# Windowed attention of the second layer: probabilities scaled ahead of their transposes, outputs kept turned

## The chip, the cores and the metric

One NeuronCore of a Trainium2 chip runs the whole program in one launch. The metric is the device time of one execution in microseconds (us), as the median of several timed runs; lower is better. A separate execution is profiled, and all rows shown come from it.

## What is computed

A trunk of two decoder layers over 1024 tokens of width 1024, in float32. Layer 0 mixes by retention and by dilated attention, layer 1 by sliding-window attention with grouped heads and learned sinks; each layer ends in an MLP with a squared ReLU. The change lies in the mixer of layer 1:

```
h = rmsnorm(x, norm_mix[1])
q, k, v = split(h @ w_qkv + b_qkv)          # 16 query heads, 4 key/value heads, 64 wide
q, k = rope(rmsnorm(q)), rope(rmsnorm(k))
s = q . k / 8, keys at distance 0..127 only
m = max(max over keys of s, sink)
p = exp(s - m);  den = sum(p) + exp(sink - m)
o = (p @ v) / den                           # 16 heads side by side: 1024 columns
x = x + o @ w_out1
```

## The kernel before

**Tiles.** The tokens lie on the 128 partitions in T = 8 tiles. Every projection is a float32 product made of three single-pass products of high and low parts (hi x hi, lo x hi, hi x lo), so each left operand stands turned, with the model's columns on the partitions, in `hT_hi` and `hT_lo`.

**The second attention stage** is `s_slots`, one function of that name on each engine, all written out by hand as a pipeline over slots t. There are 4 groups of heads (one key/value head with its four query heads) by 8 token tiles, 32 pairs p = (group, tile). Slot t makes the projection of pair t (24 matmuls of 128x384, `gemm_steps`), and at the same time the later steps of earlier pairs. Each engine runs its instructions in the order written, and waits on semaphores:

- TensorE: 12 of the 24 projection matmuls, then `trans(t-3)`, which turns the probabilities, `scores(t-2)`, `values(t-4)`; then the other 12 matmuls, `backs(t-4)` and `heads_T(t-1)`, which turns the queries and the key.
- ScalarE: `head_squares(t)`, in four of eight slots the high half of a weight split, `copy_O(t-4)`, `probs_T(t-3)` (turned probabilities out of PSUM), `probs` for the first half of pair t-2 (exponentials), `probs` for the second half, `heads_T_copy`.
- VectorE: `bias_G(t)` (evacuates the projection), `outputs(t-5)`, in four of eight slots `split_lo` (the low half of a weight split), `sums(t-1)` (sums of the squares), `maxima` of the first half of pair t-2 (mask, maximum, sink), `prep(t-1)` (norm and rotation), `maxima` of the second half.
- GpSimd: `gains(t)`, `keep_V(t-3)`, `head_rstd(t-1)` (a power to -1/2 of five numbers, L1949).

`values` multiplies V by the turned probabilities and so gives the output turned (head columns on the partitions, `o_ps`). Before, `copy_O` writes it to `Pm`, `backs` turns it back with two transposes, and `outputs` multiplies it by 1/den into `X`. For the output projection the finished tile of `X` is then turned again: `mixed_T` (eight transposes a tile, six tiles inside the slots from t = 30 on, and two more by `tile_T` in `out_proj`), copied and split by `copy_half` and `lo_half`.

In the first slots of a group a pair's keys are only one block wide (`width` is 128 in place of 256), so slots with t = 2, 3, 4 modulo 8 have less work on TensorE. From t = 32 on the slots carry the first column block of the output projection; `X` is loaded again from `x_spill` for the residual.

The lines that the prediction steps on: L498 to L500 projection matmuls, L567 transposes of probabilities, L615 scores, L644 values, L603 transposes back, L541 transposes of the finished tile, L651 turned heads; on ScalarE L1010 and L1013 exponentials, L1020 and L1022 copies of the turned heads, L965 squares; on VectorE L1647 evacuation, L1588 to L1592 `outputs`, L1636 `split_lo`, L1500 `sums`, L1574 to L1582 `maxima`, L1509 to L1526 `prep`; on GpSimd L1933 `gains`, L1949 the power.

Of the kernel before, what the change touches and what calls it, by code (L numbers as in the profile page):

```python
# [29 lines left out]
def hybrid_trunk(nc, x_in, positions, norm_mix, norm_mlp, w_up, w_down, w_in, w_out0, gn_gain, dq_gain, dk_gain,  # L30
# [59 lines left out]
    with ctx:  # L90
# [125 lines left out]
        half_out = [tp[:, 0:512], tp[:, 512:1024]]  # L216
        o_backs = o_ps[:, 256:512]
# [23 lines left out]
        half_T, half_hi, half_lo = [sem(n) for n in ("half_T", "half_hi", "half_lo")]  # L241
# [44 lines left out]
        def o_turned(kind, n):  # L286

            return qT[:, n % 2, P:2 * P] if kind == "D" else Pm[:, n, 512:512 + P]
# [16 lines left out]
        DR_SLOTS, S_SLOTS = NG * 2 * T + 2, NG * T + 4  # L305
# [6 lines left out]
        O1_T, O1_HALVES, O1_GEMMS = 30, 6, 4  # L312
# [64 lines left out]
        def _(sp):  # L377
# [63 lines left out]
            def load_mlp(l, first, normed):  # L441
                for p in range(2):
                    load_tile(l, p, p, first)
                sp.wait_ge(nt_done, normed)
# [48 lines left out]
        def _(pe):  # L493
# [39 lines left out]
            def mixed_T(i, k):  # L533

                pe.wait_ge(o_evac, A_S + (NG - 1) * T + i + 1)
                pe.wait_ge(ht_ready, k + i)
                pe.wait_ge(pt_ready, U_S + min(i + O1_T - 2, NG * T))
                for h in range(2):
                    for d in range(4):
                        c = slice((4 * h + d) * P, (4 * h + d + 1) * P)  # L540
                        last = nc.tensor.transpose(half_out[h][:, d * P:(d + 1) * P], X[:, i, c], ident[:, :])  # L541
                    last.then_inc(nt_done if h else half_T, 1)

# [80 lines left out]
            def trans(p, t):  # L624
                a = p % T
                pe.wait_ge(pt_ready, U_S + p)
                if t > O1_T:
                    pe.wait_ge(ht_ready, 4 * T + min(t - O1_T, O1_HALVES))
                for j in range(2):
                    pe.wait_ge(p_ready, A_S + 2 * p + j + 1)  # L630
                    for c, to, _, _ in blocks(a):
                        last = turn(j * 256 + to // 2, Pm[:, j, c:c + P])
                last.then_inc(tp_done, 1)

            def values(p):
                a = p % T
                pe.wait_ge(pt_ready, U_S + p + 1)
                pe.wait_ge(v_ready, A_S + p + 1)
                pe.wait_ge(o_evac, A_S + p)
# [107 lines left out]
            def s_slots():  # L747

                for t in range(S_SLOTS):
# [31 lines left out]
            def out_proj(n0, slots, first, k, m, gemms, tiles, side, ready):  # L781

                for j, w in enumerate(OUTW):
                    for i in range(gemms if j == 0 else 0, T):
                        if j == 0 and tiles + i - gemms < T:
                            done, base, per = ready
                            pe.wait_ge(done, base + per * (tiles + i - gemms))
# [100 lines left out]
            out_proj(N_O0, (0, 1, 0), P_O0, T, 1, O0_GEMMS, DR_SLOTS - O0_T, 2, (r_x, NG * T, 0))  # L888
# [16 lines left out]
            out_proj(N_O1, (0, 1, 0), P_O1, 4 * T, 3, O1_GEMMS, O1_HALVES, 0, (o_evac, A_S + (NG - 1) * T + 1, 1))  # L905
# [4 lines left out]
        def _(act):  # L910
# [19 lines left out]
            def copy_T(i, k, side):  # L930
                act.wait_ge(nt_done, k + i + 1)
# [6 lines left out]
            def copy_half(i, h):  # L938
                act.wait_ge(nt_done if h else half_T, 4 * T + i + 1 if h else i + 1)
                A(hT_hi[:, 4 * h:4 * h + 4, i * P:(i + 1) * P], half_out[h].rearrange("p (d c) -> p d c", d=4),  # L940
                  ACT.Copy).then_inc(ht_hi if h else half_hi, 1)
# [63 lines left out]
            def probs(n):  # L1005
# [5 lines left out]
                for e in range(2):  # L1011
                    z = slice(z0 + e, z0 + e + 1)
                    last = A(Pm[:, j, e * 256:e * 256 + w], Pm[:, j, e * 256:e * 256 + w], ACT.Exp,  # L1013
# [61 lines left out]
            def s_slots():  # L1075
                for t in range(S_SLOTS):
                    if 0 <= t - 1 < NG * T:
                        head_squares("S", t, N_S, A_S)
                    if t < NG * T and t % T in SPLIT_AT:
                        p, c = SPLIT_AT[t % T], t // T  # L1080
                        split_hi(p, 1 - c % 2, W, F_S + (c + 1) * 32 * KQ + 16 * KQ * (p // 2 + 1))
                    if 0 <= t - 4 < NG * T:
                        copy_O(t - 4)
                    if 0 <= t - 3 < NG * T:
                        probs_T(t - 3)
                    if 0 <= t - 2 < NG * T:
                        probs(2 * (t - 2))
                    if t >= O1_T:
                        copy_half(t - O1_T, 0)
                        copy_half(t - O1_T, 1)  # L1090
                        reload(t - O1_T, spill)
                    if 0 <= t - 2 < NG * T:
                        probs(2 * (t - 2) + 1)
                    if 0 <= t - 1 < NG * T:
                        heads_T_copy("S", t, A_S)
# [206 lines left out]
            for i in range(O1_HALVES, T):  # L1302
                copy_T(i, 4 * T, 0)
                reload(i, spill)
            act.wait_ge(o_evac, A_S + NG * T)
# [6 lines left out]
        def _(dve):  # L1312
# [96 lines left out]
            def lo_half(i, h):  # L1409
                dve.wait_ge(ht_hi if h else half_hi, 4 * T + i + 1 if h else i + 1)  # L1410
                c = slice(i * P, (i + 1) * P)
                E.tensor_tensor(hT_lo[:, 4 * h:4 * h + 4, c], half_out[h].rearrange("p (d c) -> p d c", d=4),
                                hT_hi[:, 4 * h:4 * h + 4, c].bitcast(f32), ALU.subtract).then_inc(ht_ready if h else half_lo, 1)
# [15 lines left out]
            def normed(m, i, k):  # L1429
# [4 lines left out]
                if i >= 2:  # L1434
                    dve.wait_ge(nt_done, k + i - 1)
# [127 lines left out]
            def maxima(n):  # L1563
# [3 lines left out]
                dve.wait_ge(tp_done, U_S + p)  # L1567
# [4 lines left out]
                for e in range(2):  # L1572
                    o = e * 512 + j * 256
                    step.did(E.tensor_tensor_reduce(out=Pm[:, j, e * 256:e * 256 + w], in0=sc[:, o:o + w],  # L1574
# [9 lines left out]
            def outputs(p):  # L1584
                gg, a = p // T, p % T
                z = slice(4 * (p % 3), 4 * (p % 3) + 4)
                dve.wait_ge(ot_done, A_S + p + 1)
# [62 lines left out]
            def s_slots():  # L1650
                for t in range(S_SLOTS):
                    if 1 <= t <= NG * T:
                        bias_G(t)
                    if t == 5:

                        dve.wait_ge(spilled, 16 * T)
                    if 0 <= t - 5 < NG * T:
                        outputs(t - 5)
# [3 lines left out]
                    if 0 <= t - 1 < NG * T:  # L1662
                        sums("S", t - 1, A_S)
# [8 lines left out]
                    if t >= O1_T:  # L1672
                        lo_half(t - O1_T, 0)
                        lo_half(t - O1_T, 1)
                outputs(NG * T - 1)
# [201 lines left out]
            out_proj(N_O1, 4 * T, 3, 48, O1_GEMMS, O1_HALVES, 0)  # L1877
# [6 lines left out]
        def _(pool):  # L1884
# [17 lines left out]
            def gained(m, i, k, done):  # L1902
# [4 lines left out]
                if i >= 2:  # L1907
                    pool.wait_ge(nt_done, k + i - 1)
# [262 lines left out]
```

## Time and profile before

| | |
|---|---|
| median of 3 timed runs | 2289.47 us (2287.64 to 2290.06) |
| the profiled execution's own time | 2292.28 us, its span 2290.5 us |
| TensorE busy over the span | 2247.3 us (98%), mean granted clock 0.999 |
| VectorE busy | 1432.8 us (63%) |
| GpSimd busy | 1083.8 us (47%) |
| ScalarE busy | 833.0 us (36%) |
| `s_slots` with the rest of the first column block | about 1283 to 1558 us of the span |

The profiled execution lies 2.8 us above the median of the runs. A timeline row reads: start in us, duration in us, engine, line, operation, output<-input, shapes, count, and in brackets how long the engine was idle before it and who released it. Durations overlap on one engine (the next instruction starts before the last has drained), so costs are best taken from start to start.

### The profile page before, as it was taken

To read this page: it belongs to the slowest core of one execution; us is meant where nothing else is said; L and a number is where in the kernel's file an instruction comes from. 1 tells how busy PE (TensorE), PEld (TensorE's weight loads), DVE (VectorE), ACT (ScalarE), POOL (GpSimd) and SP (SyncE) were. 2 spreads that over 40 slices of the span, in tenths; PEclk is the share of its full clock that TensorE was granted. 3 is DMA by queue.
4 is the path that set the end of the run, shared out by engine and by line. 5 is a ranking of instruction groups with operands and counts; after the bars stand their busy time and mean duration, and the time that the engine had idled before them with its cause. 6 is when DMAs were issued, how large, how long until landed. Compare 5 with 4: busy or idle time off the path is not lost.

```text
span 2290.5 us, 35562 instructions
## 1 busy us (share of the span) xinstructions
PE 2247.3 (98%) x12808; PEld 1902.8 (83%) x12808; DVE 1432.8 (63%) x2782; ACT 833.0 (36%) x1733; POOL 1083.8 (47%) x978
## 2 busy tenths in 40 slices
PE   5999999999999999999999999999999999999999
PEld 5787878789978888888887788899878888888887
DVE  6665656571485676567583677761577577567664
ACT  5625252531332223233223466651423223223320
POOL 4323333322284566557474633323266467466551
PEclk9999999999999999999999999999999999999999
DMA  4111111122101210210203211122210210221211
GB/s 129 31 28 29 29 29 29 29 83 79 59 29 61 65 62 21 73 55 18 82 28 97 71 32 32 29 72 77 74 56 19 73 55 18 73 64 43 58 37 74
DMA packets 140984, 120.41 MB, mean 53 GB/s; under 512 B 26048, under 2 KB 126912, under 8 KB 140864
## 3 DMA queue, kind: packets, MB, share of 16 engines
q1 hardware_dynamic: 133488, 103.70, 14.7%
q10 hardware_dynamic: 7376, 15.12, 1.9%
q8 instruction: 74, 1.21, 0.2%
q14 instruction: 46, 0.38, 0.1%
HBM read 110.41 MB, written 8.39 MB: 52 GB/s over the span
## 4 chain that ended last, share of the span: by engine, by line
PE 90%; DVE 5%; POOL 2%; issue 1%; ACT 1%; DMA 0%; SPq 0%; DVEq 0%; ACTq 0%; POOLq 0%
PE gp L498 15%; PE gp L500 14%; PE gp L499 14%; PE sc L500 6%; PE sc L499 6%; PE sc L498 6%; PE tp L499 3%; PE tp L498 3%; PE tp L500 3%; PE tp L567 2%; PE sc L560 2%; PE o_ps L591 2%; PE o_ps L644 1%; PE o_ps L499 1%; PE qt L499 1%
## 5 line engine op out<-in xcount | busy, mean ns | idle before, releaser
L498 PE MATMUL gp<-W_hi,hT_hi 128*128 128x384 f32 (+1 forms) x1152 | 407.8, 354 | 9.0 <-DVE hT_lo L1426 9.0
L500 PE MATMUL gp<-W_hi,hT_lo 128*128 128x384 f32 (+1 forms) x1152 | 382.9, 332 | 0.0
L499 PE MATMUL gp<-W_lo,hT_hi 128*128 128x384 f32 (+1 forms) x1152 | 381.6, 331 | 0.0
L2017 POOL TENSOR_TENSOR W_lo<-af,W_hi 128x512 fp32r<-128x512 f32 x168 | 238.0, 1417 | 283.0 <-ACT W_hi L1160 283.0
L1997 POOL TENSOR_TENSOR W_lo<-raw,W_hi 128x1024 fp32r<-128x1024 f32 x72 | 187.4, 2607 | 231.2 <-ACT W_hi L1102 218.2
L1711 DVE TENSOR_TENSOR af<-af 128x512 f32<-128x512 f32 x112 | 81.2, 725 | 300.6 <-ACT af L1143 300.6
L2017 POOL TENSOR_TENSOR W_lo<-rb,W_hi 128x512 fp32r<-128x512 f32 x168 | 244.1, 1453 | 0.0
L498 PEld LDWEIGHTS gp<-W_hi,hT_hi 128*128 128x128 f32 x1152 | 218.7, 190 | 30.5 <-issue 23.6
L499 PEld LDWEIGHTS gp<-W_lo,hT_hi 128*128 128x128 f32 x1152 | 218.9, 190 | 0.0
L500 PEld LDWEIGHTS gp<-W_hi,hT_lo 128*128 128x128 f32 x1152 | 218.0, 189 | 0.0
L498 PE MATMUL gp<-hT_hi,W_hi 128*128 128x512 f32 x512 | 199.5, 390 | 0.0
L500 PE MATMUL gp<-hT_hi,W_lo 128*128 128x512 f32 x512 | 199.2, 389 | 0.0
L499 PE MATMUL gp<-hT_lo,W_hi 128*128 128x512 f32 x512 | 199.2, 389 | 0.0
L498 PE MATMUL sc<-hT_hi,W_hi 128*128 128x512 f32 x512 | 199.2, 389 | 0.0
L499 PE MATMUL sc<-hT_lo,W_hi 128*128 128x512 f32 x512 | 199.2, 389 | 0.0
L500 PE MATMUL sc<-hT_hi,W_lo 128*128 128x512 f32 x512 | 199.2, 389 | 0.0
L1160 ACT ACTIVATE W_hi<-af 128x512 fp32r<-128x512 f32 x168 | 105.8, 630 | 165.1 <-PE sc L500 89.3
L1892 POOL TENSOR_TENSOR W_lo<-raw,W_hi 128x768 fp32r<-128x768 f32 (+1 forms) x54 | 95.6, 1776 | 137.4 <-ACT W_hi L921 109.1
L1143 ACT ACTIVATE af<-gp 128x512 f32<-128x512 f32 x56 | 33.5, 598 | 347.5 <-PE gp L500 347.5
L498 PEld LDWEIGHTS sc<-hT_hi,W_hi 128*128 128x128 f32 x512 | 96.1, 188 | 20.0
L499 PEld LDWEIGHTS sc<-hT_lo,W_hi 128*128 128x128 f32 x512 | 96.1, 188 | 20.0
L500 PEld LDWEIGHTS gp<-hT_hi,W_lo 128*128 128x128 f32 x512 | 96.1, 188 | 20.0
(305 smaller groups left out, 5095.0 us busy)
## 6 DMA issues: line engine op xcount, KB each, us to landing
raw<-in_mlp_w_up SPq DMA_DIRECT2D x64, 512.0 KB, 4.1
rb<-in_mlp_w_down SPq DMA_DIRECT2D x56, 512.0 KB, 5.5
raw<-in_hyb_w_in SPq DMA_DIRECT2D x74, 128.0 KB, 2.4
X<-in_x SPq DMA_DIRECT2D x8, 512.0 KB, 7.8
X<-in_x ACTq DMA_DIRECT2D x8, 512.0 KB, 3.5
raw<-in_mlp_w_down SPq DMA_DIRECT2D x8, 512.0 KB, 3.5
raw<-in_swa_w_qkv SPq DMA_DIRECT2D x16, 256.0 KB, 2.9
x_spill<-X ACTq DMA_DIRECT2D x8, 512.0 KB, 2.7
```

The lines of the kernel that those rows point to most:

```text
L498: mm(o, a[0], b[0], start=first, stop=False)
L499: mm(o, a[0], b[1], start=False, stop=False)
L500: return mm(o, a[1], b[0], start=False, stop=last)
L560: last = mm(sc[:, h * 512:h * 512 + w], qT[r, a % 2, 0:P], kT[r, c * 512:c * 512 + w], start=True, stop=True)
L567: last = nc.tensor.transpose(tp[:, qh * 512 + to:qh * 512 + to + HD], block[r, :], ident[r, r])
L591: last = mm(o_ps[r, 0:P], V[:, b, r], halves(pT[:, c, :], h * 256 + x // 2), start=b == 0, stop=b == a)
L1143: A(af[:, i, sh * 512:(sh + 1) * 512], u_out[n % U_BANKS], ACT.Relu).then_inc(u_evac, 1)
L1160: A(WF_hi[:, op_at(side, 2 * p + k)], x(k), ACT.Copy).then_inc(op_hi, 1)
L1711: E.tensor_tensor(x, x, x, ALU.mult).then_inc(a_sq, 1)
L1892: E.tensor_tensor(W_lo[:, slot, c], raw[:, p % 2, 0:n], W_hi[:, slot, c].bitcast(f32), ALU.subtract).then_inc(w_ready, 1)
L1997: E.tensor_tensor(WF_lo[:, at], raw[:, j % 2, :], WF_hi[:, at].bitcast(f32), ALU.subtract).then_inc(w_ready, 1)
L2017: E.tensor_tensor(WF_lo[:, c], x(k), WF_hi[:, c].bitcast(f32), ALU.subtract).then_inc(op_ready, 1)
```

## The change

The division by den moves ahead of the transposes. A new step `scale(p)` on VectorE forms 1/den as soon as the exponentials of a pair are done and multiplies the four blocks of probabilities (128x256 each) in place. The output of `values` is then final and is already turned, so `copy_O` writes it straight into `X`, which holds the turned tile, and `backs`, `outputs` and `mixed_T` are gone. `hi_turned` and `lo_turned` make `hT_hi` and `hT_lo` from `X` in SBUF, with no transpose. `Pm` gets two alternating halves (`Pm_at`). Scaling takes a slot more, so `trans` and `values` run one slot later, and there are 37 slots in place of 36, with five projection tiles of the output inside them. `sums` stands directly behind `bias_G` on VectorE, with `scale` behind it and `split_lo` after that; on ScalarE `heads_T_copy` stands ahead of the second `probs`. The reload of a tile of `X` waits for its `lo_turned`.

```
@@ tensor
-            def backs(p):
-                pe.wait_ge(ot_copied, A_S + p + 1)
-                for j in range(2):
-                    last = nc.tensor.transpose(o_backs[:, j * P:(j + 1) * P], o_turned("S", j), ident[:, :])
-                last.then_inc(ot_done, 1)
...
-            def trans(p, t):
+            def trans(p):
                 pe.wait_ge(pt_ready, U_S + p)
-                if t > O1_T:
-                    pe.wait_ge(ht_ready, 4 * T + min(t - O1_T, O1_HALVES))
+                pe.wait_ge(p_scaled, 4 * (p + 1))
...
-                    if 0 <= t - 3 < NG * T:
-                        trans(t - 3, t)
+                    if 0 <= t - 4 < NG * T:
+                        trans(t - 4)
                     if 0 <= t - 2 < NG * T:
                         scores(t - 2)
-                    if 0 <= t - 4 < NG * T:
-                        values(t - 4)
+                    if 0 <= t - 5 < NG * T:
+                        values(t - 5)
...
-                    if t >= O1_T:
-                        mixed_T(t - O1_T, 4 * T)
                     next(steps)
-                    if 0 <= t - 4 < NG * T:
-                        backs(t - 4)
@@ scalar
+            def hi_turned(i):
+                A(hT_hi[:, :, i * P:(i + 1) * P], x_turned(i), ACT.Copy).then_inc(ht_hi, 1)
...
-                A(Pm[:, :, 512:512 + P], o_ps[:, 0:2 * P].rearrange("p (j n) -> p j n", j=2), ACT.Copy).then_inc(ot_copied, 1)
+                A(X[:, p % T, bass.ds(p // T * 2 * P, 2 * P)], o_ps[:, 0:2 * P], ACT.Copy).then_inc(ot_copied, 1)
@@ vector
+            def lo_turned(i):
+                dve.wait_ge(ht_hi, 4 * T + i + 1)
+                c = slice(i * P, (i + 1) * P)
+                E.tensor_tensor(hT_lo[:, :, c], x_turned(i), hT_hi[:, :, c].bitcast(f32), ALU.subtract).then_inc(ht_ready, 1)
...
-            def outputs(p):
...
-                dve.wait_ge(ot_done, A_S + p + 1)
+            def scale(p):
+                w = width(p % T)
...
+                dve.wait_ge(p_ready, A_S + 2 * p + 2)
                 step.did(E.tensor_tensor(den[:, z], den[:, z], es[:, z], ALU.add))
                 step.wait()
                 step.did(E.reciprocal(rden[:, z], den[:, z]))
                 step.wait()
-                E.tensor_tensor(X[:, a, bass.ds(gg * 4 * HD, 4 * HD)].rearrange("p (e d) -> p e d", e=4),
-                                o_backs.rearrange("p (e d) -> p e d", e=4),
-                                rden[:, z].rearrange("p (e o) -> p e o", o=1).to_broadcast([P, 4, HD]), ALU.mult).then_inc(o_evac, 1)
+                for j in range(2):
+                    for e in range(2):
+                        x = Pm_at(p, j, e * 256, w)
+                        k = z0 + 2 * j + e
+                        E.tensor_scalar(x, x, rden[:, k:k + 1], None, ALU.mult).then_inc(p_scaled, 1)
```

**VectorE's order**, in a slot with a split in the middle of the stage. Names: `Pm` probabilities, `sc` scores in PSUM, `st` small statistics, `G` the evacuated projection. Before:

```order
L1647 SCALAR_TENSOR_TENSOR G<-gp,st,nlm 128x384
L1588 TENSOR_TENSOR st<-st 128x4
L1590 RECIPROCAL st<-st 128x4
L1592 TENSOR_TENSOR X<-o_ps,st 128x256
L1636 TENSOR_TENSOR W_lo<-raw,W_hi 128x768
L1500 TENSOR_REDUCE st<-sq 128x5
L1574 ISA Pm,st<-sc,c 128x256
```

and after the change:

```order
L1644 SCALAR_TENSOR_TENSOR G<-gp,st,nlm 128x384
L1494 TENSOR_REDUCE st<-sq 128x5
L1583 TENSOR_TENSOR st<-st 128x4
L1585 RECIPROCAL st<-st 128x4
L1591 TENSOR_SCALAR Pm<-Pm,st 128x256 x4
L1633 TENSOR_TENSOR W_lo<-raw,W_hi 128x768
L1568 ISA Pm,st<-sc,c 128x256
```

The sums went from behind the outputs and the split to directly behind the evacuation; one product of 128x256 out of PSUM became four products in SBUF, and these and the split now stand behind the sums.

**ScalarE's order**, one slot without a split. Before:

```order
L1010 ACTIVATE st<-st 128x2
L1013 ACTIVATE Pm,st<-Pm,st 128x256 x2
L1010 ACTIVATE st<-st 128x2
L1013 ACTIVATE Pm,st<-Pm,st 128x256 x2
L1020 ACTIVATE qT<-qt 128x256
L1022 ACTIVATE kT<-qt 128x128
L965 ACTIVATE sq<-G 128x320
```

and after:

```order
L1001 ACTIVATE st<-st 128x2
L1005 ACTIVATE Pm,st<-Pm,st 128x256 x2
L1012 ACTIVATE qT<-qt 128x256
L1014 ACTIVATE kT<-qt 128x128
L1001 ACTIVATE st<-st 128x2
L1005 ACTIVATE Pm,st<-Pm,st 128x256 x2
L956 ACTIVATE sq<-G 128x320
```

The two copies of the turned heads moved ahead of the second pair of exponentials; the squares still stand behind both.

## Rows read from the trace of the kernel before

**Rows 1.** Stages: window, its length, busy time of PE, PEld, DVE, ACT, POOL, clock, DMA

```profile
1403.00:1462.00 59.00, 59.00 (x537) 52.59 (x536) 45.53 (x188) 36.79 (x125) 22.34 (x32) 1.00 0.10 28
```

**Rows 2.** Timeline of TensorE, ends of slots in the middle of the stage

```profile
1348.77 0.38 PE L603 MATMUL o_ps<-ident,Pm 128*128 128x128 f32 x2
...
1400.30 0.38 PE L603 MATMUL o_ps<-ident,Pm 128*128 128x128 f32 x2
...
1407.82 0.38 PE L603 MATMUL o_ps<-ident,Pm 128*128 128x128 f32 x2
1408.04 0.49 PE L651 MATMUL qt<-ident,QK 128*128 128x128 f32 x3
1408.28 0.42 PE L498 MATMUL gp<-W_hi,hT_hi 128*128 128x384 f32 x1
```

**Rows 3.** Timeline of TensorE, one finished tile turned

```profile
1541.73 1.03 PE L541 MATMUL tp<-ident,X 128*128 128x128 f32 x8
...
1542.52 0.42 PE L498 MATMUL gp<-W_hi,hT_hi 128*128 128x384 f32 x1
...
1542.78 0.34 PE L499 MATMUL gp<-W_lo,hT_hi 128*128 128x384 f32 x1
```

**Rows 4.** Timeline of VectorE, one slot without a split

```profile
1404.85 0.42 DVE L1574 CUSTOM_DVE_ANT_0 Pm<-sc,c 128x256 f32<-128x256 f32 x1 [1.12 <-PE sc L615]
...
1405.95 0.49 DVE L1509 TENSOR_TENSOR QK<-QK,st 128x320 f32<-128x320 f32 x1
...
1407.44 0.42 DVE L1574 CUSTOM_DVE_ANT_0 Pm<-sc,c 128x256 f32<-128x256 f32 x1
...
1408.58 0.62 DVE L1647 SCALAR_TENSOR_TENSOR G<-gp,st,nlm 128x384 f32<-128x384 f32 x1
1409.11 0.15 DVE L1588 TENSOR_TENSOR st<-st 128x4 f32<-128x4 f32 x1
...
1409.51 0.42 DVE L1592 TENSOR_TENSOR X<-o_ps,st 128x256 f32<-128x256 f32 x1
1410.76 0.49 DVE L1500 TENSOR_REDUCE st<-sq 128x5 f32<-128x320 f32 x1 [0.83 <-ACT sq L965]
```

**Rows 5.** Timeline of ScalarE, the same slot

```profile
1408.64 0.20 ACT L1010 ACTIVATE st<-st 128x2 f32<-128x2 f32 x1 [0.55 <-DVE st L1582]
...
1409.74 0.36 ACT L1020 ACTIVATE qT<-qt 128x256 f32<-128x256 f32 x1
...
1410.16 0.46 ACT L965 ACTIVATE sq<-G 128x320 f32<-128x320 f32 x1
```

**Rows 6.** Timeline of VectorE, a weight split in the next slot

```profile
1416.64 1.12 DVE L1636 TENSOR_TENSOR W_lo<-raw,W_hi 128x768 fp32r<-128x768 f32 x1
```

**Rows 7.** Timeline of VectorE in the first attention stage: a product by a column, later one by a constant

```profile
504.33 0.26 DVE L1458 TENSOR_SCALAR QK<-rQK,st 128x64 f32<-128x64 f32 x1
...
504.66 0.22 DVE L1464 TENSOR_SCALAR re<-re 128x128 f32<-128x128 f32 x1
```

**Rows 8.** Line L1869: duration in ns (min/median/max), start, form

```profile
L1869 DVE TENSOR_SCALAR c<-c x1: 284/284/284, 1247.2 to 1247.2; 128x256 f32<-128x256 f32 x1
```

**Rows 9.** Timelines of GpSimd and VectorE: one beside the other

```profile
84.57 2.28 POOL L1892 TENSOR_TENSOR W_lo<-raw,W_hi 128x768 fp32r<-128x768 f32 x1 [3.33 <-DVE st L1550]
85.05 1.82 DVE L1399 TENSOR_SCALAR st<-st 128x4 f32<-128x4 f32 x1
...
1305.99 1.52 POOL L1933 TENSOR_TENSOR QK<-G,c 128x320 f32<-128x320 f32 x1 [3.61 <-DVE G L1647]
...
1411.73 1.17 POOL L1949 TENSOR_TENSOR st<-st 128x5 f32<-128x5 f32 x1
...
1412.50 0.16 DVE L1580 TENSOR_TENSOR st<-st 128x2 f32<-128x2 f32 x1
```

**Rows 10.** Stages at the start of `s_slots`: columns as in rows 1

```profile
1285.00:1290.00 5.00, 3.02 (x18) 2.69 (x16) 2.48 (x10) 0.47 (x1) 2.27 (x3) 1.00 0.01 3
1290.00:1295.00 5.00, 4.91 (x24) 4.25 (x25) 1.05 (x3) 1.64 (x4) 2.25 (x3) 0.66 0.00 0
```

More of the change, by code:

```diff
@@ L240, in hybrid_trunk @@
             sem(n) for n in ("ss_ready", "rstd_ready", "xn_ready", "nt_done", "ht_hi", "ht_ready")]
-        half_T, half_hi, half_lo = [sem(n) for n in ("half_T", "half_hi", "half_lo")]
+        p_scaled = sem("p_scaled")
         gemm_done, gemm_evac = sem("gemm_done"), sem("gemm_evac")
@@ L286, in o_turned, with turned, x_turned, Pm_at @@
         def o_turned(kind, n):
-            return qT[:, n % 2, P:2 * P] if kind == "D" else Pm[:, n, 512:512 + P]
+            return qT[:, n % 2, P:2 * P]
+        def turned(k):
+            return k - T if k >= 5 * T else k
+        def x_turned(i):
+            return X[:, i, :].rearrange("p (d c) -> p d c", d=KD)
+        def Pm_at(p, j, c, w):
+            c += p % 2 * 512
+            return Pm[:, j, c:c + w]
         def both(x, w):
@@ L443, in load_mlp @@
                     load_tile(l, p, p, first)
-                sp.wait_ge(nt_done, normed)
+                sp.wait_ge(nt_done, turned(normed))
                 for q in range(NQ):
@@ L531, in gemm_steps @@
                     yield
[L533 to L542, printed above, removed]
             def nothing():
@@ L785, in out_proj @@
                         if j == 0 and tiles + i - gemms < T:
-                            done, base, per = ready
-                            pe.wait_ge(done, base + per * (tiles + i - gemms))
+                            pe.wait_ge(*ready)
                             tile_T(X[:, tiles + i - gemms, :], tiles + i - gemms, k, side)
@@ L930, in copy_T @@
             def copy_T(i, k, side):
-                act.wait_ge(nt_done, k + i + 1)
+                act.wait_ge(nt_done, turned(k) + i + 1)
                 A(hT_hi[:, :, i * P:(i + 1) * P], nt_out[side][i].rearrange("p (d c) -> p d c", d=KD),
@@ L1012, in probs @@
                     z = slice(z0 + e, z0 + e + 1)
-                    last = A(Pm[:, j, e * 256:e * 256 + w], Pm[:, j, e * 256:e * 256 + w], ACT.Exp,
+                    x = Pm_at(n // 2, j, e * 256, w)
+                    last = A(x, x, ACT.Exp,
                              scale=-1.0, bias=negm[:, z], accum_out=den[:, z])
@@ L1081, in s_slots @@
                         split_hi(p, 1 - c % 2, W, F_S + (c + 1) * 32 * KQ + 16 * KQ * (p // 2 + 1))
+                    if t == 5:
+                        act.wait_ge(spilled, 16 * T)
+                    if 0 <= t - 5 < NG * T:
+                        copy_O(t - 5)
                     if 0 <= t - 4 < NG * T:
-                        copy_O(t - 4)
-                    if 0 <= t - 3 < NG * T:
-                        probs_T(t - 3)
+                        probs_T(t - 4)
+                    if t > O1_T:
+                        reload_turned(t - 1 - O1_T)
+                    if t >= O1_T:
+                        act.wait_ge(ot_copied, A_S + (NG - 1) * T + t - O1_T + 1)
+                        hi_turned(t - O1_T)
                     if 0 <= t - 2 < NG * T:
                         probs(2 * (t - 2))
[L1088 to L1091, printed above, removed]
+                    if 0 <= t - 1 < NG * T:
+                        heads_T_copy("S", t, A_S)
                     if 0 <= t - 2 < NG * T:
                         probs(2 * (t - 2) + 1)
-                    if 0 <= t - 1 < NG * T:
-                        heads_T_copy("S", t, A_S)
             def gain_load(dst, v):
@@ L1301, in _ @@
             s_slots()
[L1302 to L1305, printed above, removed]
+            act.wait_ge(ot_copied, A_S + NG * T)
+            hi_turned(T - 1)
+            for i in (T - 2, T - 1):
+                reload_turned(i)
             gain_load(gA, norm_mlp[1])
@@ L1434, in normed @@
                 if i >= 2:
-                    dve.wait_ge(nt_done, k + i - 1)
+                    dve.wait_ge(nt_done, turned(k) + i - 1)
                 E.scalar_tensor_tensor(xn[:, i % 2, :], X[:, i, :], rstd[:, i:i + 1], gain[:, :], ALU.mult,
@@ L1573, in maxima @@
                     o = e * 512 + j * 256
-                    step.did(E.tensor_tensor_reduce(out=Pm[:, j, e * 256:e * 256 + w], in0=sc[:, o:o + w],
+                    step.did(E.tensor_tensor_reduce(out=Pm_at(p, j, e * 256, w), in0=sc[:, o:o + w],
                                                     in1=swm[:, 256 - w:256], scale=1.0, scalar=3e38, op0=ALU.add,
@@ L1653, in s_slots @@
                         bias_G(t)
[L1654 to L1658, printed above, removed]
+                    if 0 <= t - 1 < NG * T:
+                        sums("S", t - 1, A_S)
+                    if 0 <= t - 3 < NG * T:
+                        scale(t - 3)
                     if 1 <= t <= NG * T and (t - 1) % T in SPLIT_AT:
@@ L1672, in s_slots @@
                     if t >= O1_T:
-                        lo_half(t - O1_T, 0)
-                        lo_half(t - O1_T, 1)
-                outputs(NG * T - 1)
+                        lo_turned(t - O1_T)
+                lo_turned(T - 1)
             def out_proj(n0, k, m, full, gemms, tiles, side):
@@ L1907, in gained @@
                 if i >= 2:
-                    pool.wait_ge(nt_done, k + i - 1)
+                    pool.wait_ge(nt_done, turned(k) + i - 1)
                 E.tensor_tensor(nbuf[m][0][:, i % 2, :], X[:, i, :], nbuf[m][1][:, :], ALU.mult).then_inc(xn_ready, 1)
```

38 lines of the change are left out of this document (15 added, 23 removed).

## The prediction

> **What bounds the kernel now.** I read the views from coarse to fine. The stages first: in the middle of the second attention stage TensorE is busy for all 59 of 59 us, VectorE for 45.5 and GpSimd for 22.3 [rows 1]. So TensorE alone sets the pace there, and each instruction taken from it is worth its full time until something else becomes as slow. TensorE's timeline gives the pace: 7.52 us from the end of one full slot to the next (1400.30 to 1407.82), and 59.05 us for eight slots (1348.77 to 1407.82), because the three with a narrow first pair are shorter [rows 2]. Then VectorE's and ScalarE's timelines of the same slot [rows 4, 5], for what stands in a ring: the work that each must finish before it can begin the same work of the next slot.
>
> **What TensorE gives back.** The two transposes back start at 1407.82 and the next step at 1408.04: 0.22 us [rows 2], 32 times, 7.0 us. Eight transposes of a finished tile last from 1541.73 to 1542.52, and the first matmul behind them takes 0.26 us to its successor, some 0.09 more than others: 0.88 us [rows 3], for 8 tiles 7.0 us. If TensorE stayed the bound the kernel would be 14.1 us faster, with slots of 7.30 us. The one slot more costs nothing by itself: its 24 matmuls came out of the loop behind it.
>
> **What VectorE gets.** Per pair it loses the product out of PSUM and keeps the sum and the reciprocal (0.40 us from 1409.11 to 1409.51 [rows 4]). It gains four products of 128x256 in SBUF by a column. No row shows that form. By a constant it takes 0.284 us [rows 8]; start to start an instruction of this kind takes some 0.08 less than its listed duration (504.33 to 504.66 holds two listed at 0.26 and 0.25 [rows 7], 0.17 each), so 0.20. Multiplying by a column costs more: 64 columns take 0.26 against 0.22 for 128 by a constant [rows 7], and with 0.03 for the missing 64 columns the column's surcharge is some 0.06. I take 0.26 each, 1.04 us for four. The bounds are 0.20 (no surcharge) and 0.35 (the pace of the 128x256 instruction out of PSUM, 1404.85 [rows 4], 0.42 less the overlap).
>
> The Trainium skill (VectorE: DVE Perf Modes, section on the TRN2 errata) gives 58 cycles plus half the elements at 0.96 GHz for such an instruction, an estimate of 0.19 us. By that price the sum below would end some 6 us lower than at 0.26, near no change.
>
> **The ring through VectorE and ScalarE.** Take the end of the second `maxima` as the start, 1408.58. ScalarE's second exponentials begin when they are done and last until 1409.74: 1.16 us. The copies of the turned heads no longer stand in between. The squares and their hand-over to the sums take 0.60 (1410.16 to 1410.76) [rows 4, 5]. The evacuation on VectorE (0.53) is over long before that, so with `sums` directly behind it VectorE now sits idle for about 1.2 us in each slot, where before it did the outputs and the split. Then follow, all in series now: sums 0.42, sum and reciprocal 0.40, four products 1.04, first maxima 1.10 (1404.85 to 1405.95), `prep` 1.49 (to 1407.44), second maxima 1.14 (to 1408.58) [rows 4]. The ring is 1.16 + 0.60 + 0.42 + 0.40 + 1.04 + 1.10 + 1.49 + 1.14 = 7.35 us. In the four slots of eight with a split its 1.04 us (1.12 less the overlap [rows 6]) stands in the ring too: 8.39 us. Before, the same ring held neither products nor split, but the copies (0.42): 6.3 us, hidden below 7.52 (1.16 + 0.42 + 0.60 + 0.42 + 1.10 + 1.49 + 1.14).
>
> TensorE cannot run ahead of it: `heads_T` waits for `prep`, and its queue holds the next slot's matmuls behind that wait. So a slot lasts as long as the longer of TensorE's 7.30 and the ring: 7.35 without a split (before 7.52), 8.39 with one. The first pair of a group has half width in maxima (four times 0.13), exponentials and products, about 1.0 us less, though TensorE's floor gives part of this up. Eight slots: 4 x 7.35 + 4 x 8.39 - 0.7 = 62.3 us, against 59.0. Over the 28 slots t = 5 to 32 this is 28/8 x 3.3 = +11.5; against it, the transposes of three finished tiles fall into slots 30 to 32 of before (-2.6), while `lo_turned`, about 1.3 us between the second maxima and the next evacuation, reaches past ScalarE's part of the ring by 0.7 in slots 31 and 32 (+1.4): about +10. Slots 3 and 4, estimated at 6.8 and 7.1 us before, reach 7.8 and 8.4: +2.3. Behind slot 32 the ring is open and TensorE sets the pace: five tiles' transposes (-4.4) and the last transposes back (-0.7) are gained, and 1.6 us of `trans` and `values` come a slot later into it. That is -3.5. Together +9 us.
>
> **The edits that I cost at nothing.** `hi_turned` (one copy for two) stands in ScalarE's idle time before `probs`; the reloads wait for `lo_turned` of the slot before, long done, and their data is wanted two slots on; if a load came later, the residual's addition would wait and with it a PSUM bank. The first matmuls of the output projection want `lo_turned` two slots earlier. ScalarE waits for `spilled` as VectorE did.
>
> **GpSimd beside the products.** GpSimd's power takes 1.17 us [rows 9] and begins 0.97 us after the sums start, now in the midst of the four products. The rows show that the two engines block each other: a 128x4 product took 1.82 us on VectorE and ended when GpSimd's split of 2.28 us did, and GpSimd's `gains` took 1.52 in place of 0.88 us beside VectorE's split [rows 9]. If the power waits until the products are through, it ends 1.86 + 1.17 + 0.1 = 3.13 us after the sums begin, where `prep` would like to start at 2.96: +0.17 in most slots, some 3 to 4 us. I count 3. The sum is **+12 us**: 2292.3 + 12 = 2304.3 for a profiled execution, and against the median, which lies 2.8 us below it, 2289.5 + 12 = **2301.5 us**.
>
> **Rivals.**
>
> 1. *The power holds the products up* (0.12). If it gets between the first and the second product and keeps them out for its 1.17 us, the ring grows by about 1.1 us in 30 slots, +33: 2334 us; half of it, 2318. Against it: VectorE's 128x2 instruction with two inputs took 0.16 us in the middle of such a power [rows 9], so at least its reading is not kept out. By the Trainium skill (SBUF — State Buffer, section "SBUF: two separate sides") whichever starts first holds the shared pair of ports for the whole instruction; the 1.82 us row agrees with that, the 0.16 us row does not.
> 2. *The products are cheap* (0.14). At 0.20 us the ring is 7.11 and 8.15 us; slots without a split fall to TensorE's 7.30. The sum is +3: 2292.5 us, no change that can be told. For it speaks only the row by a constant.
> 3. *Faster* (0.09). The ring does not close as I draw it: it decides only if a slot with a split comes in under 7.5 us, 0.9 less than my sum. The place would be ScalarE: were the squares done before the second exponentials came, or these much shorter, VectorE's 1.2 us of idle time would go, the split slots fall to 7.3, and the transposes' 14.1 us be gained whole, 2275.4 us; with half of the wait left, about 2283. Against it: the squares stand behind the exponentials in ScalarE's order.
> 4. *The change does not bring sums earlier at all*: true in my sum. They start where the squares allow, 2.2 us after the second maxima before and 1.8 now. Should the copies of the heads be late (they now stand ahead of the exponentials), the ring would go through TensorE's `heads_T`: before, turned heads were ready about when the second maxima ended, so this costs 0.2 us a slot at most, +6 in all: 2307. It lies in my range.
> 5. *The clock* (0.05). At the stage's start 2 us of waiting in 5 were followed by a mean granted clock of 0.66 over the next 5 us, a stretch at 1.2 in place of 2.4 GHz [rows 10]. TensorE will now wait 1.1 us in a slot of 8.4, much less densely. If it fell once in each split slot for 2 us, 16 x 1 = +16: 2318 us.
>
> **How the numbers follow.** My forecast has 0.60, with its own bounds at the product's price: +4 to +20 (0.35 us each adds 0.09 x 4 x 30 = 11 us). The range reaches from rival 2's lower side to halfway into rivals 1 and 5: 2288 to 2324 us. A measurement of this kernel can tell 0.2%, 4.6 us, from no change. Slower by more holds the forecast but for its lowest end, and rivals 1 and 5: 0.75. Within it: rival 2 and that end, 0.17. Faster: 0.08.
>
> **What would show it.** Right: VectorE idle about 1.2 us before the sums in every slot, released by ScalarE's squares; TensorE idle about 1 us before `heads_T`, released by `prep`, in slots with a split and nearly nothing in the others; slots of 8.4 and 7.4 us; the four products 1.0 to 1.1 us. Wrong: TensorE busy throughout with slots of 7.30 us (rival 3), products of 0.2 us (rival 2), a product stretched to over 1 us beside GpSimd's power (rival 1), or a clock below 1.00 in the stage (rival 5).

## The result and the profile after

The changed kernel took a median of 2296.02 us (2293.11 to 2296.69, 8 runs), the kernel before 2289.39 us (2286.91 to 2290.38, 8 runs): a ratio of 1.0024, 95% interval 1.0016 to 1.0032. It is slower by 6.6 us by the medians, by 3.7 to 7.3 us by the interval, where 12 were forecast: right in direction and inside the range, about half in size.

From the page of the profile after, its busy time and the first line of its chain of waits:

```profile
span 2291.4 us, 35383 instructions
...
PE 2238.4 (98%) x12680; PEld 1887.6 (82%) x12680; DVE 1445.5 (63%) x2872; ACT 837.5 (37%) x1727; POOL 1074.7 (47%) x978
...
PE 87%; DVE 8%; POOL 2%; issue 1%; ACT 1%; DMA 1%; SPq 0%; DVEq 0%; ACTq 0%; POOLq 0%
```

VectorE's share of the chain has grown from 5% to 8%. The profiled execution itself took 2293.11 us, the fastest of its eight, while that of before, 2292.28, lay above all eight of its kernel's. The spans of the two therefore differ by only 0.9 us. Marks on the timelines show where the rest is: ahead of the changed stage the profiled execution of after ran 4.5 to 5 us early (the first turned heads start at 1285.60, before at 1290.09); the lead arises in the first 60 us of the program, far ahead of the changed stage (rows at the end of the section on the prediction). So the stage is measured between its own marks:

```
stretch                                          before            after             difference
slots t = 2 to 4                                 21.29             23.21             +1.92
slots t = 5 to 32                                209.86            216.45            +6.59
behind slot 32, to the norm of the next stage    82.47             79.27             -3.20
together                                                                             +5.3
```

The window in the middle of the stage, which answers to [rows 1]:

```profile
core 0: us, PE busy (x) PEld busy (x) DVE busy (x) ACT busy (x) POOL busy (x), PEclk, DMA share, GB/s
1403.00:1462.00 59.00, 56.14 (x508) 48.14 (x507) 47.66 (x203) 36.08 (x117) 19.75 (x32) 1.00 0.10 28
```

TensorE is no longer busy throughout: 56.14 of 59 us, at a granted clock of 1.00. It has lost the bound. The starts of the turned heads show the slots (the last column in brackets is what it waited for):

```profile
1340.25 0.55 PE L645 MATMUL qt<-ident,QK 128*128 128x128 f32 x3
...
1401.57 0.53 PE L645 MATMUL qt<-ident,QK 128*128 128x128 f32 x3
...
1408.89 0.54 PE L645 MATMUL qt<-ident,QK 128*128 128x128 f32 x3
...
1423.54 0.55 PE L645 MATMUL qt<-ident,QK 128*128 128x128 f32 x3
1431.75 0.55 PE L645 MATMUL qt<-ident,QK 128*128 128x128 f32 x3 [0.95 <-DVE QK L1520]
```

Eight slots take 61.32 us (1340.25 to 1401.57), before 59.05 [rows 2]. A full slot without a split takes 7.32 (1401.57 to 1408.89), one with a split 8.21 (1423.54 to 1431.75), at whose end TensorE waits 0.95 us for `prep`. VectorE's timeline of the first of them, which answers to [rows 4]:

```profile
1402.70 0.62 DVE L1644 SCALAR_TENSOR_TENSOR G<-gp,st,nlm 128x384 f32<-128x384 f32 x1
1404.38 0.49 DVE L1494 TENSOR_REDUCE st<-sq 128x5 f32<-128x320 f32 x1 [1.06 <-ACT sq L956]
1404.79 0.15 DVE L1583 TENSOR_TENSOR st<-st 128x4 f32<-128x4 f32 x1
...
1405.19 1.14 DVE L1591 TENSOR_SCALAR Pm<-Pm,st 128x256 f32<-128x256 f32 x4
1406.24 0.42 DVE L1568 CUSTOM_DVE_ANT_0 Pm<-sc,c 128x256 f32<-128x256 f32 x1
...
1407.33 0.49 DVE L1503 TENSOR_TENSOR QK<-QK,st 128x320 f32<-128x320 f32 x1
...
1420.04 0.95 DVE L1633 TENSOR_TENSOR W_lo<-raw,W_hi 128x768 fp32r<-128x768 f32 x1
1420.90 0.42 DVE L1568 CUSTOM_DVE_ANT_0 Pm<-sc,c 128x256 f32<-128x256 f32 x1
```

VectorE idles 1.06 us before the sums (1.14 in most full slots), for ScalarE's squares; four products last 1.05 us start to start; `prep` follows the first maxima with no wait. The last two rows are the split of a later slot: it holds VectorE for 0.86 us. GpSimd's timeline of the same slot, and the power of a later slot whose four products are only 128x128:

```profile
1403.40 0.88 POOL L1926 TENSOR_TENSOR QK<-G,c 128x320 f32<-128x320 f32 x1 [4.17 <-DVE G L1644]
1404.21 0.25 POOL L1934 COPY V<-G 128x64 f32<-128x64 f32 x1
1405.07 0.20 POOL L1940 TENSOR_SCALAR st<-st 128x5 f32<-128x5 f32 x1 [0.61 <-DVE st L1494]
1405.35 1.22 POOL L1942 TENSOR_TENSOR st<-st 128x5 f32<-128x5 f32 x1
...
1419.40 1.17 POOL L1942 TENSOR_TENSOR st<-st 128x5 f32<-128x5 f32 x1
```

The gains are over before the sums begin, and the power (L1942) starts in the midst of the products, and does not wait until they are through. Beside four products of 128x256 it takes 1.21 or 1.22 us in 26 slots, in the six others, beside narrower products or none, 1.17 or 1.18. The wide products lengthen it by 0.04 to 0.05 us, and in the slot shown `prep` starts 0.76 us after it has ended. Over the stage, the waits of all engines (us in total, times, longest):

```profile
DVE st L1494 <- ACT sq L956: 34.0, 31, 1.2
...
PEld qt L645 <- DVE QK L1520: 23.4, 25, 2.4
...
PE qt L645 <- DVE QK L1520: 15.7, 16, 2.1
```

### The profile page after: what moved, and what is told of

Same layout as the page of the kernel before. It is cut to its first block, busy times and chain, and to the rows that moved or that the text cites. A ratio compares the mean times of both kernels' runs of the same rounds, so it can differ in the third digit from the quotient of the medians.

```text
span 2291.4 us, 35383 instructions
## 1 busy us (share of the span) xinstructions
PE 2238.4 (98%) x12680; PEld 1887.6 (82%) x12680; DVE 1445.5 (63%) x2872; ACT 837.5 (37%) x1727; POOL 1074.7 (47%) x978
## 4 chain that ended last, share of the span: by engine, by line
PE 87%; DVE 8%; POOL 2%; issue 1%; ACT 1%; DMA 1%; SPq 0%; DVEq 0%; ACTq 0%; POOLq 0%
PE gp L509 14%; PE gp L511 13%; PE gp L510 13%; PE sc L511 6%; PE sc L510 6%; PE sc L509 6%; PE tp L510 3%; PE tp L509 3%; PE tp L511 3%; PE tp L567 2%; PE sc L560 2%; PE o_ps L591 2%; PE qt L510 1%; PE o_ps L510 1%; PE o_ps L509 1%
```

## The experiments

The theory after the result: a slot lasts as long as the longer of TensorE's 7.30 us and a ring through VectorE and ScalarE, in which scaling and split stand in series behind the sums, while VectorE idles ahead of them. Rivals: TensorE's own work still decides, or GpSimd's branch (sums, power, `prep`) does, or what the products do to GpSimd. All kernels are edits of the changed one. Slot times are read as above; "eight slots" always begins at the eighth turned heads of the stage, and the last two columns are slots of full width in its middle.

```
kernel           median  of before  ratio [95% interval]       eight slots  no split  split
(changed)        2296.02 2289.39    1.0024 [1.0016, 1.0032]    61.32        7.33      8.20
e1_split_first   2283.16 2290.13    0.9972 [0.9960, 0.9985]    58.44        7.34      7.42
e2_sums_last     2309.36 2290.13    1.0082 [1.0065, 1.0099]    65.05        7.76      8.62
e3_copies_last   2304.73 2290.13    1.0059 [1.0040, 1.0078]    64.60        7.77      8.63
e4_halves        2288.60 2291.18    0.9986 [0.9977, 0.9996]    59.41        7.32      7.79
e5_both          2283.79 2291.18    0.9966 [0.9952, 0.9979]    58.20        7.32      7.42
e6_narrow        2286.89 2291.18    0.9979 [0.9970, 0.9988]    59.32        7.31      7.71
e7_more_turns    2299.40 2290.13    1.0043 [1.0026, 1.0060]    62.00        7.56      8.20
```

**The split ahead of the sums**

```diff
+                    if 1 <= t <= NG * T and (t - 1) % T in SPLIT_AT:
+                        c = (t - 1) // T
+                        split_lo(P_S + 4 * (c + 1), SPLIT_AT[(t - 1) % T], 1 - c % 2)
                     if 0 <= t - 1 < NG * T:
                         sums("S", t - 1, A_S)
                     if 0 <= t - 3 < NG * T:
                         scale(t - 3)
-                    if 1 <= t <= NG * T and (t - 1) % T in SPLIT_AT:
-                        c = (t - 1) // T
-                        split_lo(P_S + 4 * (c + 1), SPLIT_AT[(t - 1) % T], 1 - c % 2)
```

> The weight split stands between the evacuation and the sums, in VectorE's idle time; nothing else differs from the changed kernel. If the ring through VectorE and ScalarE sets the slots, the split leaves it (0.53 + 1.04 us fit into the 1.76 us until the sums can start): slots with a split fall from 8.20 to 7.35 us, 16 of them, 2283 to 2284 us. If instead the split slots are long for another reason (weights' loads, GpSimd held up), they stay at 8.2 us and the time at 2296 us.

Measured: 2283.16 us, 7.0 below the kernel before. VectorE and GpSimd in a slot with a split (e1_split_first):

```profile
1420.05 0.95 DVE L1633 TENSOR_TENSOR W_lo<-raw,W_hi 128x768 fp32r<-128x768 f32 x1
1421.42 0.49 DVE L1494 TENSOR_REDUCE st<-sq 128x5 f32<-128x320 f32 x1 [0.43 <-ACT sq L956]
...
1420.21 1.52 POOL L1926 TENSOR_TENSOR QK<-G,c 128x320 f32<-128x320 f32 x1 [3.98 <-DVE G L1644]
...
1422.11 0.20 POOL L1940 TENSOR_SCALAR st<-st 128x5 f32<-128x5 f32 x1 [0.20 <-DVE st L1494]
```

The same instructions in another order: the split now fills idle time (0.43 us of it is left here, 0.20 to 0.43 in such slots), and slots with a split fall from 8.20 to 7.42. GpSimd's gains grow to 1.52 us beside the split, and nobody waits for it. So it was the place of the split that made the change slower. This version is faster than both kernels, by the intervals of the table.

**The sums last again, behind scaling and split**

```diff
-                    if 0 <= t - 1 < NG * T:
-                        sums("S", t - 1, A_S)
                     if 0 <= t - 3 < NG * T:
                         scale(t - 3)
...
+                    if 0 <= t - 1 < NG * T:
+                        sums("S", t - 1, A_S)
```

> Undoes one part alone: the sums stand behind the split again, and the scaling directly behind the evacuation. If only VectorE's order and its idle time counted, the scaling would start 0.6 us earlier and slots would be 7.30 and 7.7 us, 2287 us. If GpSimd's power, which prep waits for, is a second branch of the ring, it ends 2.27 us after the sums start, and slots are 7.5 to 7.6 and 8.4 to 8.5 us: 2302 to 2304 us.

Measured: 2309.36 us. VectorE and GpSimd (e2_sums_last):

```profile
1405.92 1.14 DVE L1591 TENSOR_SCALAR Pm<-Pm,st 128x256 f32<-128x256 f32 x4
1406.98 0.48 DVE L1494 TENSOR_REDUCE st<-sq 128x5 f32<-128x320 f32 x1
1409.22 0.49 DVE L1503 TENSOR_TENSOR QK<-QK,st 128x320 f32<-128x320 f32 x1 [0.62 <-POOL st L1942]
...
1407.94 1.17 POOL L1942 TENSOR_TENSOR st<-st 128x5 f32<-128x5 f32 x1
```

Here GpSimd's branch does close the ring: 0.62 us of waiting before `prep`, every slot 0.4 longer, 6 us worse than the theory's figure. That is because scaling ahead of the sums waits for the exponentials (19.5 us in 29 waits over the stage), which I had not counted. So the third part of the change, the sums up front, is worth about 13 us under the other two (against the changed kernel's +6.6, this one's +19.2). It also gives a control: no GpSimd instruction lies beside these products, and they take 1.14 us as listed, what they take beside the power in the changed kernel. The power takes 1.17 us here, beside no product, in 31 of 32 slots.

**The copies of the heads behind the second exponentials**

```diff
+                    if 0 <= t - 2 < NG * T:
+                        probs(2 * (t - 2) + 1)
                     if 0 <= t - 1 < NG * T:
                         heads_T_copy("S", t, A_S)
-                    if 0 <= t - 2 < NG * T:
-                        probs(2 * (t - 2) + 1)
```

> Undoes one part alone: ScalarE copies the turned heads behind the second exponentials again, as before. If the ring runs through ScalarE's queue the copies' 0.42 us stand in it: slots 7.8 and 8.6 us, about +13, 2309 us. If the squares were held up by something else than ScalarE's order, the slots stay at 7.35 and 8.20 and the time at 2296 us.

Measured: 2304.73 us, slots of 7.77 and 8.63. VectorE's wait for the squares (e3_copies_last, one slot):

```profile
1405.28 0.49 DVE L1494 TENSOR_REDUCE st<-sq 128x5 f32<-128x320 f32 x1 [1.59 <-ACT sq L956]
```

It has grown by about what the copies take, from 1.06 to 1.59 us in this slot and from 1.14 to 1.58 in most full ones, and each slot by 0.43: ScalarE's share of the ring was as drawn. The whole came out 4 us lower than expected, but its four executions lie in two pairs (2301.3 and 2302.4, 2307.1 and 2307.9 us), and the profiled one, 2307.09, is of the upper pair; this run sizes the slots and not the whole.

**More work for TensorE**

```diff
-                for j in range(2):
+                for j in (0, 1, 1):
```

> TensorE turns the second half of each pair's probabilities twice, to the same place with the same data: 0.27 us more work for it per slot. If the ring is the bound, slots with a split stay at 8.2 us and the others grow from 7.35 to TensorE's 7.57: +3, 2299 us. If TensorE is still the bound everywhere, every slot grows by 0.27: +8.6, 2304 to 2305 us.

Measured: 2299.40 us. Slots with a split stay at 8.20, although TensorE has 0.27 us more to do in each; only the others grow, 7.33 to 7.56. TensorE has slack in the first kind and almost none in the second, as the theory has it. Together with e1_split_first this rules out that TensorE's own work bounds the slots with a split.

**Half of the scaling ahead of the sums**

```diff
-            def scale(p):
+            def scale(p, halves=(0, 1)):
...
-                dve.wait_ge(p_ready, A_S + 2 * p + 2)
+                dve.wait_ge(p_ready, A_S + 2 * p + halves[-1] + 1)
...
+                    if 0 <= t - 3 < NG * T:
+                        scale(t - 3, (0,))
                     if 0 <= t - 1 < NG * T:
                         sums("S", t - 1, A_S)
                     if 0 <= t - 3 < NG * T:
-                        scale(t - 3)
+                        scale(t - 3, (1,))
```

> The scaling is cut in two: the first half (sum and reciprocal of two columns, two products) stands between the evacuation and the sums of squares, where VectorE idles about 1.06 us waiting for ScalarE's squares; the second half and the split stay behind the sums. Theory A (the ring decides, and products pass beside GpSimd's gains as they pass beside its power): two products, 0.53 us, leave the ring; the second half's sum and reciprocal cost what the whole's did. Slots without a split fall from 7.35 to TensorE's 7.30, slots with one from 8.20 to about 7.67; eight slots 61.3 - 2.3 = 59.0 us, 28 slots -8: 2288 us. Theory B (GpSimd's gains, started ahead of the products, hold them up for the rest of its 0.88 us): the first half ends about 0.4 to 0.5 us after the squares are ready, nearly all of the gain is lost: split slots about 8.1 us, 2295 us.

Measured: 2288.60 us, theory A's time. The two halves of one scaling on VectorE, and GpSimd beside them (e4_halves):

```profile
1408.82 1.07 DVE L1592 TENSOR_SCALAR Pm<-Pm,st 128x256 f32<-128x256 f32 x2
1409.80 0.48 DVE L1494 TENSOR_REDUCE st<-sq 128x5 f32<-128x320 f32 x1
...
1410.58 0.62 DVE L1592 TENSOR_SCALAR Pm<-Pm,st 128x256 f32<-128x256 f32 x2
...
1408.59 0.88 POOL L1929 TENSOR_TENSOR QK<-G,c 128x320 f32<-128x320 f32 x1 [3.88 <-DVE G L1645]
1409.42 0.30 POOL L1937 COPY V<-G 128x64 f32<-128x64 f32 x1
...
1410.76 1.20 POOL L1945 TENSOR_TENSOR st<-st 128x5 f32<-128x5 f32 x1
```

Both expectations were half right. Theory B's mechanism is there: two products that start behind GpSimd's gains take 1.07 us, the same two beside its power 0.62. But the idle time is long enough to take in most of this, and the sums start 1.91 us after the evacuation does, where in the changed kernel it is 1.76 (1409.96 to 1411.72). These 0.15 us are about the 0.12 by which slots with a split (7.79) lie above theory A's 7.67.

**Both: split ahead in its slots, half of the scaling in the others**

```diff
+                    cut = 1 <= t <= NG * T and (t - 1) % T in SPLIT_AT
+                    if cut:
+                        split_lo(P_S + 4 * (c + 1), SPLIT_AT[(t - 1) % T], 1 - c % 2)
+                    elif 0 <= t - 3 < NG * T:
+                        scale(t - 3, (0,))
                     if 0 <= t - 1 < NG * T:
                         sums("S", t - 1, A_S)
                     if 0 <= t - 3 < NG * T:
-                        scale(t - 3)
-                    if 1 <= t <= NG * T and (t - 1) % T in SPLIT_AT:
-                        c = (t - 1) // T
-                        split_lo(P_S + 4 * (c + 1), SPLIT_AT[(t - 1) % T], 1 - c % 2)
+                        scale(t - 3, (0, 1) if cut else (1,))
```

> Slots with a split: the split stands ahead of the sums, in VectorE's idle time, and the whole scaling behind them (as in e1_split_first). Other slots: half of the scaling ahead of the sums, half behind (as in e4_halves). Theory A: slots with a split 7.35 to 7.43 us as in e1, the others at TensorE's 7.30 in place of 7.35: about 0.7 to 1 us below e1, 2282.4 us. Theory B (the gains hold up the products of the first half): the slots without a split grow by 0.2 to 0.4 us, 14 of them +3 to +5: 2286 to 2288 us, slower than e1.

Measured: 2283.79 us, 7.4 below the kernel before as measured beside it, where e1_split_first lay 7.0 below its own: no difference that these runs can tell. Eight slots are 0.24 us shorter, by theory A, but one slot of the last group takes 7.77 us in place of 7.42, and the last two slots, in which the outputs' low halves stand between maxima and evacuation, take 8.00 and 8.08 in place of 7.92 each. There is little more to gain from VectorE's order in the middle: TensorE is busy for 58.65 of 59 us (e5_both, columns as above), and the eight slots of 58.20 us are 0.9 above an estimate for TensorE alone, 59.06 less eight times 0.22.

```profile
1403.00:1462.00 59.00, 58.65 (x526) 51.49 (x526) 53.74 (x224) 38.00 (x126) 22.65 (x32) 1.00 0.10 28
```

**Narrow products**

```diff
-                        x = Pm_at(p, j, e * 256, w)
+                        x = Pm_at(p, j, e * 256, 8)
```

> The changed kernel with each of the four products over 8 columns in place of 256; this leaves out the scaling of the other columns. If the products' 1.05 us stand in the ring as drawn, they shrink to about 0.3 us (four small instructions of 0.08 each): split slots 8.20 - 0.75 = 7.45, others TensorE's 7.30, eight slots 61.3 - 3.2 = 58.1, 28 slots -11: 2285 us. If what costs were not the products but their number, or something they wait for, the slots would stay at 8.2: 2296 us. GpSimd's power, which begins 0.97 us after the sums and runs beside the products in the changed kernel at 1.17 to 1.22 us, should now take what it takes alone; 1.17 or more would say that the products never held it up, about 1.0 or less would say that they did.

Measured: 2286.89 us. Each product covers 8 columns of its block, so the other columns stay unscaled. VectorE and GpSimd (e6_narrow):

```profile
1410.36 0.65 DVE L1591 TENSOR_SCALAR Pm<-Pm,st 128x8 f32<-128x8 f32 x4
1410.93 0.28 DVE L1568 CUSTOM_DVE_ANT_0 Pm<-sc,c 128x128 f32<-128x128 f32 x1
...
1410.52 1.17 POOL L1942 TENSOR_TENSOR st<-st 128x5 f32<-128x5 f32 x1
```

The four take 0.57 us start to start, where I had expected 0.3: a product of 8 columns costs 0.14 us, not 0.08. The saving is thus 0.48 in place of 0.75, and 8.20 - 0.48 = 7.72 is what the slots with a split show (7.71). So the products stand in the ring at full price. The power takes 1.17 us here in 30 of 32 slots (once 1.18, once 1.22), against 1.21 or 1.22 beside the wide products of the changed kernel: the wide products add 0.04 to 0.05 us to it, and do not hold it up for their 1.05 us.

## Why the prediction was half right

The direction, the ring and the waits came out as forecast; the sum was about twice too large. Two of its terms failed: the wait of GpSimd's power for the products, 3 us that do not exist, and the price of the split in the ring, 1.04 us for what takes 0.86.

- **The ring decides: right.** VectorE idles 1.06 to 1.14 us before the sums (about 1.2 forecast), TensorE waits 0.95 us for `prep` where a split is (about 1 forecast). Slots without a split take 7.33 us (7.35 forecast). Moving the split out of the ring (e1), shortening the products in it (e6), adding copies to it (e3) and adding work to TensorE beside it (e7) each moved the slots as the ring says.
- **The products: right.** 0.26 each was forecast; 1.05 us for four is 0.26. The Trainium skill (VectorE: DVE Perf Modes, section on the TRN2 errata) gave an estimate of 0.19, too low. Its slope agrees with the runs: from 8 to 256 columns a product grows from 0.14 to 0.265 us, 0.5 ns a column, where half a cycle at 0.96 GHz is 0.52. The difference is in the fixed part: 58 cycles are 0.06 us, and the 8-column products take 0.14.
- **The split's price: wrong.** The prediction put "its 1.04 us (1.12 less the overlap [rows 6])" into the ring; it takes 0.86. The row that it was read from lay beside GpSimd's work, which had started ahead of it; in the changed kernel the gains are over when the split begins, and all 16 splits of the stage are listed at 0.95. Fourteen slots by 0.18 are 2.5 us too much. The trace of before held the right price too, in an earlier slot, where the split is the first to start and GpSimd's gains are the ones that stretch (kernel before, VectorE, and in [rows 9] GpSimd at 1305.99):

```profile
1305.83 0.95 DVE L1636 TENSOR_TENSOR W_lo<-raw,W_hi 128x768 fp32r<-128x768 f32 x1
```

- **GpSimd's power behind the products: wrong.** "If the power waits until the products are through ... I count 3." It does not wait: it starts 0.97 us after the sums and takes 1.21 or 1.22 us beside wide products (changed kernel), 1.17 beside narrow ones (e6) or when they are over (e2), and the products take 1.14 us with it or without. What the products add to it is 0.04 to 0.05 us, ahead of a `prep` that starts later still, so the 3 us do not exist. By the prediction's own ring they could not have fallen into "most slots" either: where a split stands between products and `prep`, `prep` starts 1.04 us later than the 2.96 that it reckoned with. Rival 1 falls with it. The prediction had the row that said so (the 0.16 us instruction in the midst of a power [rows 9]) and used it only against the rival.
- **Slots 3 and 4, the part behind slot 32: right.** +1.9 for +2.3, of which the split's price is 0.36; -3.2 for -3.5.
- **The sum.** Forecast 12. Without the power's 3 and with the split at 0.86 it is 6.5. The stage in the profiles shows 5.3, the medians 6.6. Most of the remaining 1 us is in the slots with a narrow first pair: three of them (7.06, 7.60, 8.19) are 0.9 us shorter than full ones of their kind, where the prediction took off 0.7, and the 28 slots hold 3.5 groups of eight.
- **Sums that do not follow.** Rival 2's +3 us was too low on its own terms: 0.24 us off the ring takes about 3.8 us off 16 split slots and 0.7 off the others, held at 7.30, which leaves +7.5 of the 12, or +4.5 without the power's 3. The estimate of 0.19 likewise leaves about +6, and not "near no change". The upper bound of the forecast's own span, +20, should be +23 by its 11 us. The products cost 0.26, so none of this bears on what was measured.
- **The other rivals.** Rival 2 (cheap products) and rival 3 (the ring does not close) fall by the rows above. Rival 4's late copies are nearly not seen: in the full slots looked at, the second exponentials begin 0.06 us after the evacuation does, at 1410.02 in the slot shown, as before (1408.58 and 1408.64 [rows 4, 5]); in a slot whose first pair is narrow, 0.21. Rival 5 happened once in the stage behind its first two slots: in 1310 to 1320 the granted clock is 0.83 (before 1.00), and that slot took 8.53 in place of 8.21 us, 0.3 us in all. The profiles of e2_sums_last and e3_copies_last show 0.83 in the same window, and their slots there are no longer than the others. At the stage's start, where TensorE waits about 2 us, the clock fell before and after alike (0.66 over 5 us, [rows 10] and 1285 to 1290 here), and slot 2 took 7.35 and 7.41 us; in e1_split_first and e4_halves the windows 1285 to 1290 and 1290 to 1295 show 1.00, and it took 5.87 and 5.88. That fall is worth about 1.5 us of one execution, and it is no part of what the edits do.

```profile
1310.00:1320.00 10.00, 10.00 (x70) 8.47 (x70) 7.37 (x28) 6.67 (x22) 3.34 (x6) 0.83 0.01 2
```

The lead of the profiled execution of after is there at the program's beginning. The same exponential of ScalarE starts 6.2 us earlier than before (first row the kernel before, second the changed one):

```profile
59.54 0.60 ACT L988 ACTIVATE Pm<-Pm,st 128x384 f32<-128x384 f32 x1
...
53.30 0.60 ACT L979 ACTIVATE Pm<-Pm,st 128x384 f32<-128x384 f32 x1
```

In the window 40 to 50 the clock is 0.83 before and 1.00 after; in 505 to 515 it is 0.83 after and 1.00 before, behind which the lead is 4.8 us. In the profiles of the seven edits the same exponential is 0.9 to 3.0 us earlier than before. What decides this scatter at the start stays open; the marks inside the stage do not need it.

Of the 14.1 us that TensorE gives back, e1_split_first realises 7.0. In slots 5 to 32 TensorE gives back 8.8 (28 times 0.22 and three tiles of 0.88), and this kernel is 3.9 shorter there (205.97 against 209.86). The rest went in the slots with a narrow first pair (7.05, 7.37, 7.14, against an estimate for TensorE alone of 6.90, 7.04, 6.86), in full slots of 7.31 to 7.42 in place of 7.30, and in the last two of 7.92. Which wait ends last in each of these was not read.

## What to carry to other kernels

When a change takes work from the engine that sets the pace, draw the ring through the others and ask where in it that engine's partners idle: work moved from behind a wait to before it is free, and here the place of one subtraction (the split) decided between 6.6 us lost and 7.0 us won. Take a duration from a row whose neighbours on the other engines are those that it will have after the change, and look for its shortest and longest row before using it. The contention seen here between wide instructions was no price for a narrow one: look for a row with the narrow one in it.

## What the runs showed of the hardware

- VectorE's and GpSimd's wide instructions on SBUF hold each other up in these rows, and the one that starts first keeps its time. The split (128x768) started first takes 0.95 us and the gains (128x320) 1.52; with the gains started first they take 0.88, two products behind them 1.07 in place of 0.62, and the split 1.12 [rows 6]. By the Trainium skill (SBUF — State Buffer, section "SBUF: two separate sides") whichever starts first holds the shared port pair for its whole instruction, and these rows agree in which of the two is held up.
- GpSimd's power of 128x5 is outside this: it does not wait for the products, which lengthen it from 1.17 to 1.21 or 1.22 us, and it does not delay them (1.14 us for four of 128x256 with it or without). By that rule of the Trainium skill, whichever started first should have held the other up.
- A product of VectorE by a column in SBUF costs, start to start, 0.14 us at 8 columns, 0.20 at 128 (1419.24 to 1420.04 for four, in the changed kernel) and 0.265 at 256. Four of them narrowed to 8 columns still cost over half of the wide ones.
